# Three of four query and key chunks of the first block computed by seven half-size products each

## The chip, the core and the metric

The kernel runs on one core of one Trainium2 chip. Its engines are PE (TensorE, the matrix engine), DVE (VectorE), ACT (ScalarE), POOL (GpSimd) and SP (SyncE, which here only issues DMAs); each runs its own list of instructions in order, and semaphores tie them together. The metric is the device time of one launch in microseconds (us), the median of several runs.

## The reference, cut to what matters

The kernel computes two transformer blocks on 512 tokens of width 1024, in float32. The first is differential attention followed by a mixture of experts, the second a Fourier and neighbourhood-attention mixer. The change touches the first projection of the first block:

```
xn = x * rsqrt(mean(x*x, -1) + 1e-6) * gain          # [512, 1024]
q, k, v = split(xn @ w_in, [1024, 2048])             # w_in [1024, 3072]
q = rmsnorm per head of 64 (q, q_gain) * 64**-0.5    # 8 heads x 2 x 64
k = rmsnorm per head of 64 (k, k_gain)
...
# in the second block, the same kind of product for its own input
sh, sc, g = split(silu(c) @ w_ada + b_ada)           # modulation, also computed early here
q, k, v, f_in, f_gate, na_gate = split(xn2 @ w_in2)
```

A chunk is 512 columns of `w_in`: two chunks are q (q0, q1), two are k (k0, k1), two are v.

## The kernel before, in words

The order of each engine's work is written out by hand; nothing is scheduled by a planner. `x` comes in four tiles of 128 tokens. PE transposes a tile (`h_transposes`), DVE copies it out of PSUM times the gain into `hT` (`h_copies`), and DVE, ACT and POOL work out the row factor `rstd` from the sum of squares (`norm1`, `norm1_power`). `hT` itself stays without `rstd`, which is applied to every product later.

The projection is 24 units (`unit(i)`), a unit being one chunk times one token tile: 8 matmuls of 128x128 by 128x512 into one of two PSUM banks called "mm" (L824). Units 0 to 15 are q and k, units 16, 17 the first of v; the other six are fed in between the steps of the attention. Behind each q or k unit ACT squares it (L1345), DVE sums the squares by head (L1693) and adds the epsilon (L1698, L1702), POOL takes the power -1/2 (L2288), DVE scales into `pd` (L1709), and behind the next unit PE transposes `pd` (`qkT`, L795) into one of two PSUM banks called "tp"; ACT copies that into `qT` or `kT` (L1356). The scheme of the two banks: whoever wants to write the n-th tile of a kind calls `claim`, which waits until tile n-2 was drained; the bookkeeping is `turn` and `book`.

Between the units lie six steps of the modulation of the second block: `ada_rows` (8 matmuls on a `w_ada` chunk of 2 MB, L856), which ACT copies out (L1369), and `ada` (4 small matmuls, L842), which DVE drains in `ada_out` (L1679, L1682). They use the same two tp banks as the transposes, and their places are two lists, `ADA_ROWS_AFTER` and `ADA_AFTER`. SP loads the `w_ada` chunks into ring slots 0 and 1 as these come free (L654).

The ring has six slots of 2 MB in SBUF. The six chunks of `w_in` fill them at the start (L630, L622).

The second block has the scheme that the change brings to the first. For five of its chunks (`SEVEN`) a product of 512x1024 by 1024x512 is done as seven products of half size (256x512 by 512x256, 8 matmuls of 128x128 by 128x256, L1197). DVE makes four sums of the left operand once (`row_sum`, L2060), four of each weight chunk (`half_sum`, L2049) and seven sums of the products (`block_sum`, L2073); ACT copies the first product out (L1584).

Of the kernel before, what the change touches and what calls it, by code (L numbers as in the profile page):

```python
# [7 lines left out]
ALU = mybir.AluOpType  # L8
# [52 lines left out]
W_IN, W_OUT, W_MOE = 0, 8, 10  # L61
# [6 lines left out]
ADA_ROWS_AFTER = [6, 8, 9, 11, 12, 14]  # L68
ADA_AFTER = [7, 9, 10, 12, 13, 15]
# [106 lines left out]
SUMS_BEHIND = [None, 1, 4, 3, 5, 6, 7]  # L176
Q_BLOCKS = [(1, 1), (0, 0), (0, 1), (1, 0)]
HEADS_T_BEHIND = {("v", 2): 5, ("q", 6): 6, ("q", 7): 7, ("u", 1): 8, ("u", 2): 9}
# [44 lines left out]
def build(nc, ctx, A, out):  # L223
# [3 lines left out]
    def sem(name):  # L227
# [74 lines left out]
    ada_rows = s_buf[:, 0]  # L302
# [13 lines left out]
    lam_in = s_buf[:, 1, 0, 0:4 * DH].rearrange("p (n d) -> p n d", n=4)  # L316
    lam_pr = s_buf[:, 1, 1, 0:2 * DH].rearrange("p (n d) -> p n d", n=2)
# [31 lines left out]
              ("ng", buf_d[:, 2048:4096]), ("fg", ring[:, 3, 2048:4096]))}  # L349
# [44 lines left out]
    for i in range(UNITS_FIRST):  # L394
        book("mm", "proj", i)
    for i in range(UNITS_FIRST):
        if i < TT - 1:
            book("tp", "hT", 2 * i + 2)
            book("tp", "hT", 2 * i + 3)
        if 1 <= i <= QK_CHUNKS * TT:  # L400
            book("tp", "qkT", i - 1)
        if i in ADA_AFTER:
            book("tp", "ada", ADA_AFTER.index(i))
        if i in ADA_ROWS_AFTER:
            book("tp", "ada_rows", ADA_ROWS_AFTER.index(i))
# [56 lines left out]
    for what in SEVEN:  # L462
# [23 lines left out]
    slot_of, loads = {}, [9, 9, 10, 10, 9, 9]  # L486
# [12 lines left out]
    def w_half(what):  # L499

        w = ring[:, slot_of[source[what]][0], :].rearrange("p (k n) -> p k n", k=KD)
# [4 lines left out]
    def bank(j, step):  # L506

        n = 7 * j + step - 1
        b = sc_before % 2
# [91 lines left out]
    product_done = sem("product_done")  # L601
    s_ready, t_ready = sem("s_ready"), sem("t_ready")
    p1_copied = sem("p1_copied")
    sum_done = sem("sum_done")
# [14 lines left out]
    def _(sp):  # L619
# [29 lines left out]
        def load_ada(c):  # L649
            if c >= 2:  # L650
                filled(sp, "tp", turn["tp", "ada_rows", c - 2])
            else:
                filled(sp, "mm", turn["mm", "proj", (c + 1) * TT - 1])
            sp.dma_start(ring[:, c % 2, :].rearrange("p (k n) -> p k n", k=KD),  # L654
# [13 lines left out]
        for c in range(2, ADA_CHUNKS):  # L668
            load_ada(c)
# [1823 lines left out]
```

## Time and profile before

| | us |
|---|---|
| three timed runs | 955.51, 960.42, 960.25 |
| median | 960.25 |
| the profiled execution, its own time | 955.6 |
| its span in the trace | 953.5 |
| PE busy | 928.2 (97%) |
| DVE busy | 315.1 (33%) |
| ACT busy | 217.2 (23%) |
| POOL busy | 124.2 (13%) |

The profiled execution agrees with the fastest timed run; two of the three timed runs lie 4.7 to 4.9 us above it. Times inside the trace are us from the start of the span. In the trace one matmul of float32 is two records ("x16" are 8 matmuls), a matmul's record is longer than the distance to the next since they are pipelined, so what a group costs PE is read from one start to the next. In the chain of waits each piece is given with what it really adds. The units of q, k and the first of v run from 8.8 to 163.6 us, the attention follows, then the experts (358 to 629 us), then the second block, whose seven-product stage runs from 684.5 to 807.7 us.

### The profile page before, as it was taken

How to read it: one execution, taken by the hardware profiler on the slowest of the kernel's cores; microseconds unless marked ns; L12 is line 12 of the kernel's file. 1: busy time of each engine (PE TensorE's matmuls, PEld its weight loads, DVE VectorE, ACT ScalarE, POOL GpSimd, SP SyncE). 2: the span in 40 equal slices, each digit the busy share in tenths (PEclk: the TensorE clock that was granted, in tenths of full speed). 3: DMA queues.
4: the chain of work that ended last, by engine and by line, in shares of the span. 5: the costliest groups of instructions: out<-in, count | busy, mean ns of one | idle time of the engine just before them, and what ended most of it. 6: DMA issues, size and time to landing. Idle time of an engine off the chain costs nothing.

```text
span 953.5 us, 12683 instructions
## 1 busy us (share of the span) xinstructions
PE 928.2 (97%) x5258; PEld 476.1 (50%) x5258; DVE 315.1 (33%) x744; ACT 217.2 (23%) x471; POOL 124.2 (13%) x123
## 2 busy tenths in 40 slices
PE   7999999989999999999999999999999999999998
PEld 3544444444555453333333333335588888755543
DVE  2321121345774462100110110037735533344422
ACT  2121121334554310010010010114202011632310
POOL 3222121000001201000000000023202122530000
PEclk9999999999999999999999999999999999999999
DMA  9927527306001628999999999971283103500002
GB/s 329 290 96 229 204 107 276 142 1 259 6 1 45 226 89 315 376 395 409 419 413 428 422 412 415 380 262 45 92 164 107 57 23 90 198 1 1 1 12 78
DMA packets 54233, 186.32 MB, mean 195 GB/s; under 512 B 13968, under 2 KB 14624, under 8 KB 47904
## 3 DMA queue, kind: packets, MB, share of 16 engines
q1 hardware_dynamic: 45776, 160.31, 45.1%
q0 software_dynamic: 4912, 18.36, 5.2%
q10 hardware_dynamic: 3488, 6.82, 1.9%
q8 instruction: 43, 0.70, 0.3%
q14 instruction: 14, 0.11, 0.0%
HBM read 168.70 MB, written 16.79 MB: 195 GB/s over the span
## 4 chain that ended last, share of the span: by engine, by line
PE 87%; DVE 4%; DMA 3%; ACT 2%; issue 1%; SPq 1%; POOL 1%; ACTq 0%; DVEq 0%; POOLq 0%
PE psum L1022 17%; PE psum L1197 13%; PE psum L824 12%; PE psum L1045 8%; PE psum L795 6%; PE psum L1209 6%; PE psum L922 6%; PE psum L871 4%; PE psum L883 2%; PE psum L900 2%; PE psum L1266 1%; PE psum L949 1%; PE psum L1139 1%; PE psum L1296 1%; PE psum L856 1%
## 5 line engine op out<-in xcount | busy, mean ns | idle before, releaser
L1022 PE MATMUL psum<-ring,buf_a 128*32 128x512 f32 x1536 | 167.5, 593 | 1.1 <-DVE buf_a L1940 1.1
L824 PE MATMUL psum<-ring,buf_b 128*128 128x512 f32 x288 | 130.5, 606 | 2.0 <-DMA ring<-in_da_w_in 2.0
L1022 PEld LDWEIGHTS psum<-ring,buf_a 128*32 128x32 f32 x1536 | 48.9, 110 | 110.2 <-issue 110.2
L824 PEld LDWEIGHTS psum<-ring,buf_b 128*128 128x128 f32 x288 | 54.1, 193 | 68.4 <-issue 65.9
L1045 PE MATMUL psum<-ring,buf_c 128*32 128x512 f32 x768 | 84.7, 593 | 0.0
L2288 POOL TENSOR_TENSOR qk_st<-qk_st,half 128x8 f32<-128x8 f32 x26 | 43.6, 1677 | 165.8 <-DVE qk_st L2020 68.6
L922 PE MATMUL psum<-ring,buf_b 128*128 128x512 f32 x128 | 59.8, 594 | 0.0
L1209 PE MATMUL psum<-ring,buf_b 128*128 128x512 f32 x128 | 56.2, 595 | 1.7 <-DVE buf_b L2258 1.5
L1962 DVE TENSOR_TENSOR buf_c<-buf_c,psum 128x512 f32<-128x512 f32 x12 | 13.1, 1092 | 121.6 <-PE psum L1022 61.6
L1045 PEld LDWEIGHTS psum<-ring,buf_c 128*32 128x32 f32 x768 | 23.8, 110 | 52.7 <-issue 52.7
L1940 DVE TENSOR_TENSOR buf_a<-psum,gain 128x512 f32<-128x512 f32 x24 | 15.5, 687 | 101.3 <-PE psum L795 101.3
L1388 ACT ACTIVATE s_buf<-s_buf,nmx 128x128 f32<-128x128 f32 (+3 forms) x64 | 35.4, 554 | 58.9 <-DVE nmx L1756 58.9
L871 PE MATMUL psum<-ring,buf_b 128*128 128x512 f32 x96 | 44.7, 598 | 2.6 <-DVE o_sb L1776 1.8
L1756 DVE CUSTOM_DVE_ANT_0 s_buf<-psum,g_x 128x128 f32<-128x128 f32 (+3 forms) x64 | 28.9, 489 | 45.8 <-PE psum L883 45.7
L1209 PEld LDWEIGHTS psum<-ring,buf_b 128*128 128x128 f32 x128 | 23.9, 190 | 31.9 <-issue 28.9
L2354 POOL DMA_INDIRECT buf_b<-xn_d,idx x12 | 11.4, 948 | 212.9 <-PE psum L795 194.8
L2073 DVE TENSOR_TENSOR s_buf<-s_buf,psum 128x512 f32<-128x512 f32 x31 | 21.3, 687 | 47.0 <-PE psum L1197 45.3
L1197 PE MATMUL psum<-ring,buf_a 128*128 128x256 f32 x160 | 35.8, 379 | 0.0
L1693 DVE TENSOR_REDUCE qk_st<-pT 128x8 f32<-128x512 f32 x16 | 11.0, 686 | 73.0 <-ACT pT L1345 73.0
L795 PEld LDWEIGHTS psum<-ident,pd 128*128 128x128 f32 x184 | 21.6, 141 | 26.2 <-issue 23.4
L1345 ACT ACTIVATE pT<-psum,rstd 128x512 f32<-128x512 f32 x16 | 11.0, 687 | 99.0 <-PE psum L824 99.0
L1197 PE MATMUL psum<-ring,buf_b 128*128 128x256 f32 x144 | 32.4, 379 | 0.0
(294 smaller groups left out, 1186.4 us busy)
## 6 DMA issues: line engine op xcount, KB each, us to landing
ring<-in_moe_w_gate SPq DMA_DIRECT2D x16, 2048.0 KB, 12.9
ring<-in_moe_w_up SPq DMA_DIRECT2D x16, 2048.0 KB, 12.9
ring<-in_moe_w_down SPq DMA_DIRECT2D x16, 2048.0 KB, 12.6
ring<-in_w_in SPq DMA_DIRECT2D x7, 2048.0 KB, 9.5
ring<-in_w_ada SPq DMA_DIRECT2D x6, 2048.0 KB, 8.1
ring<-in_da_w_in SPq DMA_DIRECT2D x5, 2048.0 KB, 20.3
y_d<-ring POOLq DMA_DIRECT2D x1, 5632.0 KB, 22.9
y_d<-buf_b ACTq DMA_DIRECT2D x11, 512.0 KB, 11.3
```

Source lines behind the costliest of these rows:

```text
L795: last = transpose(buf("tp", n)[:, g * P:(g + 1) * P], block_in, ident[:])
L824: last = mm(buf("mm", n), hT[:, k, t * P:(t + 1) * P], slot(W_IN + c)[:, k, :], start=(k == 0), stop=(k == KD - 1))
L871: last = mm(buf("mm", n), hT[:, k, t * P:(t + 1) * P], slot(W_IN + c)[:, k, :], start=(k == 0), stop=(k == KD - 1))
L922: last = mm(buf("mm", n), oT[:, k, t * P:(t + 1) * P], slot(W_OUT + c)[:, k, :], start=(k == 0), stop=(k == KD - 1))
L1022: last = mm(buf("mm", n)[rows, :], xgT[:, s % 4, k, rows], slot(moe_load(q, m, r))[:, k, :], start=(k == 0), stop=(k == KD - 1))
L1045: last = mm(buf("sc", n)[rows, m, :], hidT[:, s % 3, f * P + SUB * j:f * P + SUB * (j + 1)], slot(moe_load(q, 2, r), FC)[:, f, m * CH:(m + ...
L1197: last = mm(out_bank[:, a * 256:(a + 1) * 256], still, moving, start=(k == 0), stop=(k == KD // 2 - 1))
L1209: last = mm(buf("sc", n)[:, a, :], mixT[:, k, t * P:(t + 1) * P], w[:, k, :], start=(k == first), stop=(k == first + 3))
L1388: last = S.activation(sc, sc, ACT.Exp, bias=nmx[:, m % 2, c:c + 1], scale=-1.0, accum_out=den[:, m % 2, c:c + 1])
L1756: last = V.tensor_tensor_reduce(out=s_buf[:, b, c, 0:w], in0=buf("sc", n)[:, c, 0:w], in1=dist[:, 512 - w:512], scale=-2.0 ** -(h + 1), sc ...
L2073: V.tensor_tensor(two(part[out]) if dst is None else dst, two(part[left]), two(bank(j, step)), ALU.add).then_inc(sum_done, 1)
L2288: G.tensor_tensor(dst, src, half[:, 0:width], ALU.pow).then_inc(signal, 1)
```

## The change

Of the four q and k chunks the first (units 0 to 3) stays as it was. The other twelve units (q1, k0, k1) are replaced by seven products each, 21 in all, with the function of the second block, now called `seven_products(f, j)` with f = 0 for the first block. What follows from it:

- The products need the operand with `rstd` in it. So each tile of `hT` is scaled in place (`scale_rows`) once the unit that reads it is done. The factor has to lie along the free axis for that: DVE builds `ident * rstd` for the four tiles, and PE multiplies it by a matrix of ones, one matmul, behind unit 1. v needs no scale any more.
- DVE makes the sums, and squares, means and scales come at the end of a chunk, from SBUF.
- The transposes and the `ada` steps move behind products, by three new tables. The `w_ada` chunks go to ring slots 1 and 2 and are loaded from the end of the first seven products on; `w_out` goes to slots 0 and 3.
- In the first block the sums of q1 lie in `buf_d`, those of k0 and k1 in ring slot 0.
- The order of the seven products is new in both blocks: the two that need no sums first. The waits of the second block move with it (among them that of the loads of `v_win`, from the fourth product of the last chunk to the fifth).
- Two loads of expert weights change places: that of up matrix 0 is issued early, that of gate matrix 2 in its place.

```diff
-ADA_ROWS_AFTER = [6, 8, 9, 11, 12, 14]
-ADA_AFTER = [7, 9, 10, 12, 13, 15]
+ADA_ROWS_BEHIND = {("k0", 4): 0, ("k0", 7): 1, ("k1", 2): 2, ("k1", 4): 3, ("k1", 6): 4, ("unit", 16): 5}
+ADA_BEHIND = {("k0", 6): 0, ("k1", 1): 1, ("k1", 3): 2, ("k1", 5): 3, ("k1", 7): 4, ("unit", 17): 5}
-SEVEN = ("v", "q", "u", "ng", "fg")
+SEVEN = ("q1", "k0", "k1"), ("v", "q", "u", "ng", "fg")
-PRODUCTS = [("A11", "B11"), ("S2", "T2"), ("S1", "T1"), ("S3", "T3"), ("A12", "B21"), ("S4", "B22"), ("A22", "T4")]
+PRODUCTS = [("A11", "B11"), ("A12", "B21"), ("S2", "T2"), ("S1", "T1"), ("S3", "T3"), ("S4", "B22"), ("A22", "T4")]
+QK_T_BEHIND = {("q1", 2): [3], ("q1", 7): [4], ("k0", 1): [5], ("k0", 2): [6], ("k0", 3): [7], ("k0", 7): [8],
+               ("k1", 1): [9], ("k1", 2): [10], ("k1", 3): [11], ("k1", 7): [12], ("unit", 16): [13, 14],
+               ("unit", 17): [15]}
...
@@ SP
+        for c in range(ADA_CHUNKS):
+            if c == 0:
+                sp.wait_ge(product_done[0], 7)
+            elif c == 3:
+                sp.wait_ge(product_done[0], 14)
+            else:
+                filled(sp, "tp", turn["tp", "ada_rows", {1: 0, 2: 1, 4: 2, 5: 3}[c]])
...
-            sp.wait_ge(product_done, 7 * 4 + (4 if c < TT - 1 else 6))
+            sp.wait_ge(product_done[1], 7 * 4 + (5 if c < TT - 1 else 6))
...
@@ PE
+        for i in (0, 1, 2, 3, 16, 17):
+            if i == 16:
+                for j in range(len(SEVEN[0])):
+                    landed(W_IN + 1 + j)
+                    seven_products(0, j)
+                pe.wait_ge(sum_done[0], 7 * 2 + 5)
...
+            if 1 <= i < TT:
+                qk_transposes(i - 1)
+            if i == 1:
+                pe.wait_ge(diag_ready, 1)
+                mm(bank(0, 0, 6), ones[:], part["c11"], start=True, stop=True).then_inc(rstd_row_ready, 1)
+            work_behind("unit", i)
...
@@ ACT, behind each chunk's products
+            act.wait_ge(sum_done[0], 7 * j + 6)
+            first_squares(4 * j + 6, part["c12"])
+            copies_behind(what, 7)
+            act.wait_ge(sum_done[0], 7 * j + 7)
+            first_squares(4 * j + 7, part["c21"])
...
@@ DVE
+        ada_in = {("k0", 7): 0, ("k1", 0): 1, ("k1", 2): 2, ("k1", 6): 3, ("k1", 7): 4}
...
+        for i in range(TT):
+            if i < TT - 1:
+                h_copies(i + 1)
+                if i < 2:
+                    norm1(i + 1)
+            if i == 1:
+                norm1(TT - 1)
+                for n in (1, 2, 3):
+                    half_sum(0, 0, n)
+            if i == 2:
+                scale_rows(0)
+            if i == TT - 1:
+                scale_rows(TT - 1)
+                row_sum(0, 1)
+                row_sum(0, 2)
+            first_mean(i)
+            if i == 1:
+                for t in range(TT):
+                    dve.wait_ge(rstd_ready, t + 1)
+                    last = V.tensor_scalar(part["c11"][:, t * P:(t + 1) * P], ident[:], rstd[:, t:t + 1], None, ALU.mult)
+                last.then_inc(diag_ready, 1)
+            if i == 2:
+                scale_rows(1)
+            first_scale(i, buf("mm", turn["mm", "proj", i]))
+            if i == 2:
+                scale_rows(2)
...
+        for j in range(3):
+            at = 4 * j + 4
+            half_sum(0, j, 4)
...
+            block_sum(0, j, 5)
+            first_mean(at)
+            block_sum(0, j, 6)
+            ada_sums(SEVEN[0][j], 6)
+            first_scale(at, part["c22"])
+            first_mean(at + 1)
...
+            first_scale(at + 1, part["c11"])
+            first_mean(at + 2)
+            block_sum(0, j, 7)
+            first_scale(at + 2, part["c12"])
+            ada_sums(SEVEN[0][j], 7)
+            first_mean(at + 3)
+            first_scale(at + 3, part["c21"])
```

Three places of the order, as it stands in the program. The first is DVE around unit 1, before. L1660 are the copies of tile 2 into `hT`, L1654 the mean for `rstd`, L1693 and L1698 the sum of the squares of unit 1, L1709 its scaling:

```order
L1660 TENSOR_TENSOR buf_b<-psum,gain 128x4x128 x2
L1654 TENSOR_SCALAR ms<-ssq 128x1
L1693 TENSOR_REDUCE qk_st<-pT 128x8
L1698 SCALAR_TENSOR_TENSOR qk_st<-qk_st,q_scale 128x8
L1709 SCALAR_TENSOR_TENSOR pd<-psum,rstd,qk_st 128x512
```

The same stretch of DVE after, where L1801 is `half_sum` and L1890 the diagonal:

```order
L1750 TENSOR_TENSOR buf_b<-psum,gain 128x4x128 x2
L1744 TENSOR_SCALAR ms<-ssq 128x1 x2
L1801 TENSOR_TENSOR buf_d<-ring 128x1024
L1801 TENSOR_TENSOR buf_d<-ring,buf_d 128x1024
L1801 TENSOR_TENSOR ring<-ring 128x4x256
L1832 TENSOR_REDUCE qk_st<-pT 128x8
L1843 SCALAR_TENSOR_TENSOR qk_st<-qk_st,q_scale 128x8
L1890 TENSOR_SCALAR s_buf<-ident,rstd 128x128 x4
L1858 SCALAR_TENSOR_TENSOR pd<-psum,rstd,qk_st 128x512
```

Three weight sums and the four pieces of the diagonal have come in ahead of the scaling. On PE, the rows between unit 1 and unit 2 after (before, L937 was not there), with what each waits for:

```order
L928 MATMUL psum<-ring,buf_b 128x512 x2
L813 MATMUL psum<-ident,pd 128x128 [waits tp_free0,mm_free0]
L813 MATMUL psum<-ident,pd 128x128 x3
L937 MATMUL psum<-s_buf,ones 128x512 [waits diag_ready]
L928 MATMUL psum<-ring,buf_b 128x512 [waits tp_free0,mm_free0]
```

The matmul of ones stands ahead of unit 2 and waits for the diagonal. The third place is PE where k0 ends and k1 begins, after: L902 are products, L813 the transposes of piece 8, L865 is `ada_rows` 1, L851 `ada` 0:

```order
L851 MATMUL psum<-o_sb,g_x 128x2 [waits fold_ready,tp_free1,tp_free0]
L851 MATMUL psum<-o_sb,g_x 128x2 x3
L902 MATMUL psum<-ring,buf_b 128x256 [waits t_ready0,p1_copied0]
L902 MATMUL psum<-ring,buf_b 128x256 x7
L813 MATMUL psum<-ident,pd 128x128 [waits tp_free0,qk_scaled]
L813 MATMUL psum<-ident,pd 128x128 x3
L865 MATMUL psum<-ring,o_sb 32x512 [waits ada_landed0,tp_free1]
```

and DVE in the same stretch, after. L1826 is `block_sum`, L1861 `first_scale`, L1832 with L1846 `first_mean`, L1769 `ada_out`:

```order
L1832 TENSOR_REDUCE qk_st<-pT 128x8 [waits sq_ready]
L1846 TENSOR_SCALAR qk_st<-qk_st 128x8 [waits dve_done]
L1826 TENSOR_TENSOR s_buf<-s_buf,psum 128x512 [waits product_done0]
L1861 TENSOR_TENSOR pd<-s_buf,qk_st 128x512 [waits tp_full0,qk_rstd_ready]
L1769 TENSOR_TENSOR mod_sh<-psum,b_ada 128x2x4 [waits tp_full1]
L1832 TENSOR_REDUCE qk_st<-pT 128x8 [waits sq_ready]
```

The drain of `ada` 0 (L1769), which frees the tp bank that `ada_rows` 1 claims, stands behind the scaling of the third piece of k0. Before, on PE, an `ada` and the next step in its bank had a whole unit of eight matmuls between them:

```order
L842 MATMUL psum<-o_sb,s_buf 128x2 [waits fold_ready,tp_free0]
L842 MATMUL psum<-o_sb,s_buf 128x2 x3
L824 MATMUL psum<-ring,buf_b 128x512 [waits mm_free0,w_landed2]
L824 MATMUL psum<-ring,buf_b 128x512 x7
L795 MATMUL psum<-ident,pd 128x128 [waits tp_free1,mm_free1]
L795 MATMUL psum<-ident,pd 128x128 x3
L856 MATMUL psum<-ring,o_sb 32x512 [waits ada_landed1,tp_free0]
```

There DVE drained `ada` 0 ahead of everything else of the next unit.

## Rows read from the trace of the kernel before

**Rows 1.** The page's first part: engine, busy us (share), instructions.

```profile
PE 928.2 (97%) x5258; PEld 476.1 (50%) x5258; DVE 315.1 (33%) x744; ACT 217.2 (23%) x471; POOL 124.2 (13%) x123
```

**Rows 2.** The chain of waits, first units: start us, us, what.

```profile
8.76 7.97 PE psum L824 x12
...
27.07 0.44 PE psum L795 x4
27.50 5.15 PE psum L824 x12
...
42.99 6.87 PE psum L824 x16
```

**Rows 3.** Windows: stretch, length, busy by engine, PEclk, DMA share, GB/s.

```profile
9.00:11.00 2.00, 2.00 (x3) 0.94 (x4) 0.15 (x1) 0.00 (x0) 1.78 (x10) 1.00 1.06 416
42.99:163.59 120.60, 119.42 (x421) 55.84 (x421) 22.24 (x51) 22.31 (x36) 23.29 (x15) 1.00 0.51 169
```

**Rows 4.** The chain of waits, seven-product stage.

```profile
742.11 65.61 PE psum L1197 x304
```

**Rows 5.** DVE in order of time, around unit 1: start us, us, line, operation.

```profile
24.95 1.29 DVE L1660 TENSOR_TENSOR buf_b<-psum,gain 128x512 f32<-128x512 f32 x2 [1.46 <-PE psum L795]
26.15 0.14 DVE L1654 TENSOR_SCALAR ms<-ssq 128x1 f32<-128x1 f32 x1
```

**Rows 6.** DVE in order of time, sums of the second block.

```profile
692.21 1.22 DVE L2049 TENSOR_TENSOR buf_d<-ring 128x1024 f32<-128x1024 f32 x1
693.46 1.23 DVE L2049 TENSOR_TENSOR buf_d<-ring,buf_d 128x1024 f32<-128x1024 f32 x1
694.61 1.22 DVE L2049 TENSOR_TENSOR ring<-ring 128x1024 f32<-128x1024 f32 x1
695.74 0.68 DVE L2073 TENSOR_TENSOR s_buf<-s_buf,psum 128x512 f32<-128x512 f32 x1
...
723.13 1.48 DVE L2073 TENSOR_TENSOR s_buf<-s_buf,psum 128x512 f32<-128x512 f32 x2 [1.63 <-PE psum L1197]
724.53 1.22 DVE L2049 TENSOR_TENSOR ring<-ring 128x1024 f32<-128x1024 f32 x1
725.66 0.68 DVE L2019 TENSOR_REDUCE qk_st<-pT 128x8 f32<-128x512 f32 x1
726.38 0.17 DVE L2020 TENSOR_SCALAR qk_st<-qk_st 128x8 f32<-128x8 f32 x1
...
728.30 0.69 DVE L2027 TENSOR_TENSOR pd<-s_buf,qk_st 128x512 f32<-128x512 f32 x1 [1.03 <-POOL qk_st L2288]
...
731.54 0.69 DVE L2027 TENSOR_TENSOR pd<-s_buf,qk_st 128x512 f32<-128x512 f32 x1 [0.82 <-POOL qk_st L2288]
```

**Rows 7.** DVE, a small operation: group by line, busy us, mean ns.

```profile
L2012 DVE TENSOR_SCALAR buf_b<-psum,mod_g,mod_sh 128x128 f32<-128x128 f32 x16 | 5.4, 404 | 0.0
```

**Rows 8.** The chain of waits, modulation steps among the units.

```profile
85.37 8.15 DMA ring<-in_w_ada
93.52 0.14 issue
...
103.08 0.79 PE psum L842 x8
```

**Rows 9.** PE in order of time, around the same steps.

```profile
91.65 0.95 PE L842 MATMUL psum<-o_sb,s_buf 128*128 128x2 f32 x8
93.65 1.92 PE L856 MATMUL psum<-ring,o_sb 128*32 128x512 f32 x16 [1.05 <-DMA ring<-in_w_ada]
```

**Rows 10.** ACT in order of time, behind unit 16.

```profile
156.33 0.69 ACT L1334 ACTIVATE buf_a<-psum,rstd 128x512 f32<-128x512 f32 x1 [6.93 <-PE psum L824]
156.91 0.68 ACT L1356 ACTIVATE buf_d<-psum,qk_gain 128x512 f32<-128x512 f32 x1
```

**Rows 11.** SP's DMA issues in order of time, the loads of `v_win`.

```profile
797.47 15.41 SPq L763 DMA_DIRECT2D buf_a<-v_d  x32
```

**Rows 12.** DMA issues, stretch 790 to 830 us: count, KB each, us to landing.

```profile
buf_a<-v_d SPq DMA_DIRECT2D x32, 64.0 KB, 1.9
```

**Rows 13.** The chain of waits, first product that reads `v_win`.

```profile
820.37 1.09 PE psum L1296 x16
```

More of the change, by code:

```diff
@@ L399, in build @@
             book("tp", "hT", 2 * i + 3)
-        if 1 <= i <= QK_CHUNKS * TT:
+        if i >= 1:
             book("tp", "qkT", i - 1)
[L402 to L405, printed above, removed]
+    for what in SEVEN[0]:
+        for step in range(1, 8):
+            book_behind(what, step)
+    for i in (16, 17):
+        book_behind("unit", i)
     for s in range(ATTENTION_STEPS):
@@ new lines, in ada_copy, with copies_behind, first_squares @@
+        def ada_copy(c):
+            n = turn["tp", "ada_rows", c]
+            filled(act, "tp", n)
+            if c >= 2:
+                filled(act, "tp", turn["tp", "ada", c - 2])
+            drain(S.copy(ada_rows[c % 2], buf("tp", n)), "tp", n)
+        def copies_behind(*place):
+            for j in QK_T_BEHIND.get(place, []):
+                qk_copy(j)
+            if place in ADA_ROWS_BEHIND:
+                ada_copy(ADA_ROWS_BEHIND[place])
+        def first_squares(j, src):
+            if j >= 2:
+                act.wait_ge(qk_ms_ready, j - 1)
+            if j < TT:
+                act.wait_ge(rstd_ready, j + 1)
+                ins = S.activation(pT[:, j % 2, :], src, ACT.Square, scale=rstd[:, j:j + 1])
+            else:
+                ins = S.activation(pT[:, j % 2, :], src, ACT.Square)
+            ins.then_inc(sq_ready, 1)
@@ new lines, in _ @@
+        for i in range(TT):
+            n = turn["mm", "proj", i]
+            filled(act, "mm", n)
+            first_squares(i, buf("mm", n))
+            if i >= 1:
+                qk_copy(i - 1)
+        act.wait_ge(second_loaded, 10 * 16)
+        act.wait_ge(pool_consts, 2)
+        S.activation(cond_pad[:, :, 0:2], cond[:], ACT.Silu).then_inc(cond_ready, 1)
+        for j, what in enumerate(SEVEN[0]):
+            act.wait_ge(product_done[0], 7 * j + 1)
+            if j == 0:
+                act.wait_ge(rstd_row_ready, 1)
+            else:
+                act.wait_ge(qk_scaled, 4 * (j - 1) + 2)
+            S.copy(part["c11"], bank(0, j, 1)).then_inc(p1_copied[0], 1)
+            for step in (1, 2, 3, 4):
+                copies_behind(what, step)
+            act.wait_ge(sum_done[0], 7 * j + 4)
+            first_squares(4 * j + 4, part["c22"])
+            copies_behind(what, 5)
+            act.wait_ge(sum_done[0], 7 * j + 5)
+            first_squares(4 * j + 5, part["c11"])
+            copies_behind(what, 6)
+            act.wait_ge(sum_done[0], 7 * j + 6)
[3 more added lines that the diff above has]
+            first_squares(4 * j + 7, part["c21"])
@@ L1371, in norm2_squares @@
+        for i in (16, 17):
+            v_copy(i)
+            copies_behind("unit", i)
         def norm2_squares(t):
@@ new lines, in row_sum @@
+        def row_sum(f, n):
+            left, right, op = {1: ("A21", "A22", ALU.add), 2: ("S1", "A11", ALU.subtract),
+                               3: ("A11", "A21", ALU.subtract), 4: ("A12", "S2", ALU.subtract)}[n]
+            if n == 1 and f == 0:
+                dve.wait_ge(h_scaled, TT)
+            elif n == 1:
+                drained(dve, "tp", turn["tp", "x3T", 2 * (TT - 1)])
+                drained(dve, "tp", turn["tp", "x3T", 2 * (TT - 1) + 1])
+            elif n in (2, 4):
+                dve.wait_ge(s_ready[f], 1 if n == 2 else 2)
+            V.tensor_tensor(x_half[f"S{n}"], x_half[left], x_half[right], op).then_inc(s_ready[f], 1)
@@ new lines, in _, with block_sum @@
+        two = lambda ap: ap.rearrange("p (t n) -> p t n", t=2)
+        def block_sum(f, j, n, dst=None):
+            left, step, out = SUM_OF[n]
+            dve.wait_ge(product_done[f], 7 * j + step)
+            if n == 1:
+                dve.wait_ge(p1_copied[f], j + 1)
+            elif n in (2, 4):
+                dve.wait_ge(sum_done[f], 7 * j + n - 1)
+            V.tensor_tensor(two(part[out]) if dst is None else dst, two(part[left]), two(bank(f, j, step)),
+                            ALU.add).then_inc(sum_done[f], 1)
```

545 lines of the change are left out of this document (283 added, 262 removed).

## The prediction

> **What bounds the kernel now.** First the page's busy times: PE is busy 928.2 us, 97% of the span, no other engine over a third [rows 1]. So a change pays what it takes off PE's list, less what PE then waits for. Second the chain of waits over the first 60 us: it is PE and nothing else, unit behind unit with four transposes of 0.44 us between them, and a unit of eight matmuls costs 6.87 us [rows 2]. Third the window over units 4 to 17: 120.60 us, PE busy in 119.42 of them, DVE in 22.2, ACT in 22.3, POOL in 23.3 [rows 3]. All helpers have room there, but their work on one unit is a chain (square, sum, power, scale), and the changed order makes PE wait for ends of such chains. So fourth I read DVE in order of time, once where unit 1 ends [rows 5], once in the second block, where the scheme already runs [rows 6]. The sum is made against the profiled execution, 955.6 us (span 953.5), 4.65 us under the median of the runs, 960.25. Two of three timed runs lie at the upper level, and nothing in one trace says which comes; I add the difference found in the trace to the median. About 0.5%, 4.8 us, is what can be told from no change, and it is also the distance of the two levels.
>
> **What PE is relieved of.** Twelve units at 6.87 are 82.4 us. In the second block 19 products run in one piece of 65.61 us, 3.453 each, with no wait [rows 4]; 21 of them are 72.5 us. Gain 9.9 us. The sixteen transposes, six `ada_rows` (1.92) and six `ada` (0.79) stay [rows 8, 9]. New is one matmul of ones, 128x512: a sixth of 5.15, 0.86 us [rows 2], 1.0 with the change of operands around it. The wait for the third `w_ada` chunk, 1.2 us from 92.45 (91.65 + 0.79) to 93.65 [rows 8, 9], goes: it came from a load of 8.15 us issued late behind small loads; in the new order the first load starts at the end of the seventh product of q1 and is used four products, three transposes, some 15 us later, and each later one has at least 8.7 us, against 8.15. What is late next there is DVE, below.
>
> **First wait: the diagonal behind unit 1.** PE ends unit 1 and its transposes at 27.07 + 0.44 = 27.50 [rows 2] and then, ahead of unit 2, waits for four diagonal pieces. DVE's list: copies of tile 2 from 24.95, the mean at 26.15, a second such mean, so free at 26.3 [rows 5]. Then three weight sums, which take 3.53 us from the first start to the next instruction in the second block (692.21 to 695.74) [rows 6]: 29.9. Their chunk must have landed; I take it as landed, since chunk 1 is behind only 4 MB in SP's queue, and if it is late the wait grows. Then the sum of unit 1's squares, 0.72 to the next instruction, and that one, 0.1: 30.7 [rows 6]. The diagonal's four operations of 128x128 are not in the trace; nearest are the 0.40 us of a TENSOR_SCALAR of the same shape out of PSUM [rows 7] and the 0.17 of one of 128x8 [rows 6]. Four give 0.7 to 1.6; I take 1.0, nearer the small one, since the input is in SBUF. PE goes on at 31.7: **4.2 us** idle (3.9 to 4.8). Queued behind the waiting matmul are unit 2 and all else on PE, so nothing covers it. The sums could have waited: their user is the third product, 20 us later.
>
> **Second wait: the tp bank between k0 and k1.** `ada_rows` 1 claims the bank of `ada` 0, which DVE drains behind the scaling of k0's third piece. Count from the end of k0's seventh product. The fifth ended 7.8 us earlier (two products and one `ada` with 0.9). DVE then does two block sums, 1.40, one weight sum, 1.13 (723.13 to 724.53 to 725.66), a block sum of 0.6, and starts the mean of the first piece at -4.6 [rows 6]. Mean to second instruction 0.72, from there to the scaling 1.92 (726.38 to 728.30), where POOL's power is waited for, and from scaling to scaling 3.24 (728.30 to 731.54) [rows 6]. So the pieces are scaled at -2.0, +1.2 and +4.5, the drain of `ada` 0 ends at +5.3. PE arrives at +0.5, behind the transposes of piece 8: **4.8 us** idle. Bounds: 3.8, if each piece goes 0.3 us quicker, to 6, if POOL or ACT are late once. ACT makes it no shorter: its copy of `ada_rows` 1 stands ahead of the last squares, which only delays piece 11, needed 15 us later.
>
> **Small ones.** Behind k1's second product `ada_rows` 2 claims the bank of `ada` 1, drained behind a weight sum that itself waits for that product: 1.2 + 0.15 against 0.44 of transposes, 0.9 us. Behind unit 16, `ada_rows` 5 needs the first of two transposes copied by ACT, which first copies v: 0.6 and 0.7 [rows 10] against 0.87 on PE, 0.4 us. The other places have cover. The transposes of q1's first piece come 0.3 us after its scaling by the same count; that is thin, and a slip there costs what it slips. `scale_rows` and `row_sum`, 1.2 us each, end at about 51.4, the third product starts at 55.5. DVE's whole load per chunk is about 16 us of 24.
>
> **The second block.** PE has no wait in the seven-product stage [rows 4], so putting the sum-free products first can gain nothing there. It moves the 32 `v_win` loads one product, 3.45 us, later: 797.47 + 3.45 + 15.41, and 1.9 to land, is 818.2 [rows 11, 12]; the product that reads them starts at 820.37 [rows 13]. 2.1 us are left, cost 0. The swap of two expert loads changes nothing: the last of the four gate matrices is issued where it was.
>
> **Sum.** -9.9 + 1.0 + 4.2 + 4.8 + 0.9 + 0.4 - 1.2 = +0.2 us. Everything behind follows PE and only shifts. On the profiled execution 955.8, on the median **960.4 us**. The change gives PE ten microseconds and takes them back in two waits.
>
> **Rivals.** (A) The sum holds. 50%, 960.4.
>
> (B) PE's clock falls in the new idle stretches. The granted clock is 1.00 of full in every row, the 2.4 GHz level [rows 3]. Yet at the start, after PE had stood for 2 us, twelve records took 7.97 us, and the same twelve at 27.50 took 5.15 [rows 2], and from 9 to 11 us only three were begun [rows 3]: PE ran at the pace of the 1.2 GHz level, whatever the column says. The price of one such stretch is 2.8 us. Here PE would stand for 4.2 and 4.8 us, longer than anywhere in this trace once it had begun. For: that start. Against: no row shows a fall after dense work, for want of such a gap. One fall gives 963.2, two 966.0; this is the side on which the kernel is slower, and it decides if the records behind the gaps are 0.86 us apart. 27% together, a third of it for two. The Trainium skill (TensorE: Matmul & The Clock Gate, HAM oscillation) says that a matmul kernel whose waits for data are long enough falls back to the half rate after each of them and pays the warm-up again; by that rule both gaps are candidates, and no run here shows it yet.
>
> (C) One of the two waits is not there, since ada 0 is drained earlier than I count or the weight sums run in DVE's gap ahead of unit 1's end. For: DVE is idle 1.5 us there [rows 5]. Against: the written order. One gone is 955.6 to 956.2, both gone 951.4. 15% together, 3% for both.
>
> (D) The products don't run back to back in the first block, or `v_win` comes late: the 0.3 and 2.1 us of room are used up. The change then doesn't do what it says at its place; up to 2 us, 961 to 962.5. 8%.
>
> **Range and chances.** From (C) with one wait gone and some more, to (B) with two falls: 952 to 966.5. Faster by over 0.5% needs under 955.4: most of (C) and a share of (A) if the runs fall at the lower level: 14%. Slower by over 0.5%, over 965.1: two falls, one fall with a late helper, or the level of the runs: 19%. The rest, 67%, can't be told from no change.
>
> **What would show it.** In the changed kernel PE should stand behind unit 1 from 27.5 to about 31.7, ended by DVE's TENSOR_SCALAR into `s_buf`; and about 4.8 us ahead of the second `ada_rows`, ended by DVE's small sum into `mod_sh`. 21 products should cost 3.45 us each, and the attention should start at about 163.8 where it did at 163.59. A first gap under 2 us, or none ahead of the second `ada_rows`, would make the forecast wrong to the fast side; a pace of 0.86 us a record behind a gap, or waits at `qk_scaled` behind most products, to the slow side.

## The result and the profile after

The changed kernel takes 961.3 us (median of 12 runs, 960.59 to 961.75). The kernel before, run beside it, takes 955.85 us (12 runs, 953.42 to 961.43). The ratio is 1.0049, interval 1.0031 to 1.0068: half a per cent slower, at the edge of what I called no change. The time forecast, 960.4, lies 0.9 us from the time measured, but the difference forecast, +0.2 us, does not: it is +5.5 us on the medians and +5.6 us between the profiled executions (961.18 against 955.6). The median of 960.25 that I added the difference to came from three runs, two of which lay at an upper level of the kernel before; with more runs that level proves to be the rarer one (17 of 91 runs of the kernel before beside the experiments, all at 960.4 us or more; the 24 runs of the changed kernel lie within 1.6 us of each other). Two single slow runs, 1382 us of the first experiment and 1959 us of the kernel before beside it, stand outside these counts and all ratios.

The page after, first part, and its line of granted clock over 40 slices of 24 us:

```profile
span 959.1 us, 13033 instructions
PE 925.4 (96%) x5404; PEld 505.0 (53%) x5404; DVE 349.2 (36%) x789; ACT 217.8 (23%) x474; POOL 124.9 (13%) x123
PEclk9999899999999999999999999999999999999999
```

PE's busy time fell by 2.8 us only [rows 1], where 9.9 less 1.0 were expected: part of what is busy there is busy at a slower clock. One digit of the clock line is an 8. Before, all were 9.

The chain of waits after, from the transposes in unit 1 on (start us, us, what; it answers to [rows 2]):

```profile
24.98 0.02 issue
25.00 1.29 DVE buf_b L1750 x2
...
29.94 0.61 DVE qk_st L1832
...
30.65 0.88 DVE s_buf L1890 x4
31.53 0.04 issue
31.57 2.08 PE psum L937 x2
33.65 5.75 PE psum L928 x12
...
49.73 6.91 PE psum L902 x32
```

DVE is now on the chain: the sums of weights, the squares' sum, the four diagonal pieces, and then the matmul of ones (L937) at 31.57, where I had counted 31.7. But L937 takes 2.08 us, not 1.0, and the twelve records behind it (L928, L824 before) take 5.75, not 5.15 [rows 2]. Products follow at 6.91 for two, 3.455 each, as forecast.

PE in order of time after, with the idle time before a piece and what ended it, at the four new waits and at one that was there before:

```profile
31.57 2.08 PE L937 MATMUL psum<-s_buf,ones 128*128 128x512 f32 x2 [4.02 <-DVE s_buf L1890]
33.44 5.96 PE L928 MATMUL psum<-ring,buf_b 128*128 128x512 f32 x12
39.23 1.04 PE L813 MATMUL psum<-ident,x 128*128 128x128 f32 x8
...
108.80 3.64 PE L865 MATMUL psum<-ring,o_sb 128*32 128x512 f32 x16 [4.87 <-DVE mod_sh L1769]
112.37 4.13 PE L902 MATMUL psum<-ring,buf_b 128*128 128x256 f32 x16
116.34 0.60 PE L813 MATMUL psum<-ident,pd 128*128 128x128 f32 x4
...
122.75 1.92 PE L865 MATMUL psum<-ring,o_sb 128*32 128x512 f32 x16 [1.03 <-DVE mod_sh L1769]
...
157.93 1.92 PE L865 MATMUL psum<-ring,o_sb 128*32 128x512 f32 x16 [0.39 <-ACT buf_d L1403]
...
208.41 3.43 PE L951 MATMUL psum<-ring,buf_b 128*128 128x512 f32 x4 [1.80 <-DVE o_sb L1994]
```

The four waits are where they were forecast and as long: 4.02 (4.2), 4.87 (4.8), 1.03 (0.9), 0.39 (0.4). What was not in the sum is beside three of the idle times: `ada_rows` (L865) takes 3.64 us behind the wait of 4.87 and 1.92 behind the two short ones, and in the attention four records of v's projection (L951) take 3.43 us, where the kernel before had the same wait of 1.80 us and then 1.98:

```profile
203.97 1.98 PE L871 MATMUL psum<-ring,buf_b 128*128 128x512 f32 x4 [1.80 <-DVE o_sb L1776]
```

Windows of the changed kernel (stretch, length, busy PE, PEld, DVE, ACT, POOL, then PEclk, DMA share, GB/s; they answer to [rows 3], where PEclk is 1.00):

```profile
20.00:27.00 7.00, 7.00 (x24) 3.48 (x23) 3.60 (x8) 0.10 (x1) 2.22 (x2) 1.00 1.05 388
27.00:32.00 5.00, 0.98 (x6) 0.74 (x5) 4.45 (x9) 1.26 (x2) 3.40 (x3) 0.93 1.05 387
31.00:32.00 1.00, 0.43 (x1) 0.43 (x2) 0.52 (x3) 0.00 (x0) 1.00 (x1) 0.66 1.06 391
32.00:34.00 2.00, 2.00 (x3) 0.75 (x3) 0.75 (x1) 0.00 (x0) 0.46 (x1) 0.50 1.05 385
34.00:36.00 2.00, 2.00 (x5) 0.91 (x4) 0.00 (x0) 0.00 (x0) 0.00 (x0) 0.82 1.05 386
36.00:100.00 64.00, 63.95 (x297) 49.39 (x296) 37.54 (x51) 12.79 (x20) 10.00 (x7) 1.00 0.38 106
100.00:112.00 12.00, 7.13 (x36) 3.83 (x35) 5.09 (x12) 1.32 (x2) 4.73 (x3) 0.77 0.00 0
112.00:114.00 2.00, 2.00 (x10) 1.44 (x7) 0.34 (x1) 1.11 (x2) 0.00 (x0) 0.69 0.27 29
114.00:200.00 86.00, 83.91 (x382) 49.34 (x381) 25.08 (x103) 22.44 (x63) 10.25 (x7) 1.00 0.65 238
200.00:210.00 10.00, 8.20 (x28) 3.51 (x28) 4.07 (x18) 4.97 (x17) 0.00 (x0) 0.94 0.01 2
210.00:215.00 5.00, 5.00 (x17) 2.26 (x16) 2.20 (x9) 1.35 (x5) 0.00 (x0) 0.78 0.00 0
```

The granted clock falls to 0.50, the 1.2 GHz level, at the first wait. It fell before the matmul of ones began: the mean from 31 to 32 us is 0.66, which takes 0.68 us at 0.50, and L937 is there only from 31.57 on. The clock is also below 1.00 at the second wait and behind the one that ends at 208.41. By 36, 114 and 215 us it is back.

From these rows the difference of the two profiled executions comes out term by term. Waits 4.02 + 4.87 + 1.03 + 0.39 = 10.3; one of 0.2 at 74.4 us; the matmul of ones at full clock 0.9; the fall at the first wait 1.65 (from the wait's end to the next transposes 39.23 - 31.57 = 7.66, where runs without a fall, below, have 6.0 to 6.1); at the second 2.1 (116.34 - 108.80 = 7.54 against 5.42); in the attention 1.65 (from the end of this wait to the end of the next one 227.87 - 208.41 = 19.46 against 221.78 - 203.97 = 17.81; the pieces behind the four records are slow too); less 9.9 for the products, 1.05 for the DMA wait at 93.65 that is gone [rows 9], and 0.55 in the mixer, where PE's wait for a piece of DVE was 1.1 and not 1.67. The sum is +5.3, measured +5.6.

The second block's products, from the chain after (they answer to [rows 4]): they start 6.15 us later than before and what follows them, too, starts 6.15 later, so nothing was won or lost there.

```profile
690.82 6.91 PE psum L902 x32
...
698.16 41.44 PE psum L902 x192
...
826.53 1.09 PE psum L1345 x16
```

### The profile page after: what moved, and what is told of

It is laid out like the page before. It is cut to its first block, busy times and chain, and to the rows that moved or that the text cites. A ratio compares the mean times of both kernels' runs of the same rounds, so it can differ in the third digit from the quotient of the medians.

```text
span 959.1 us, 13033 instructions
## 1 busy us (share of the span) xinstructions
PE 925.4 (96%) x5404; PEld 505.0 (53%) x5404; DVE 349.2 (36%) x789; ACT 217.8 (23%) x474; POOL 124.9 (13%) x123
## 4 chain that ended last, share of the span: by engine, by line
PE 87%; DVE 6%; DMA 2%; ACT 2%; POOL 2%; issue 1%; ACTq 0%; DVEq 0%; SPq 0%; POOLq 0%
PE psum L902 19%; PE psum L1104 17%; PE psum L1127 8%; PE psum L813 6%; PE psum L1259 6%; PE psum L1004 6%; PE psum L951 5%; PE psum L928 5%; PE psum L965 2%; PE psum L982 2%; PE psum L1315 1%; PE psum L1031 1%; PE psum L1221 1%; PE psum L865 1%; POOL qk_st L2466 1%
## 5 line engine op out<-in xcount | busy, mean ns | idle before, releaser
L902 PE MATMUL psum<-ring,buf_a 128*128 128x256 f32 x320 | 71.5, 381 | 0.0
L902 PEld LDWEIGHTS psum<-ring,buf_a 128*128 128x128 f32 x320 | 60.0, 190 | 10.3 <-issue 2.5
L902 PE MATMUL psum<-ring,buf_b 128*128 128x256 f32 x288 | 65.2, 382 | 0.0
L1004 PE MATMUL psum<-ring,buf_b 128*128 128x512 f32 x128 | 59.8, 594 | 0.0
L902 PEld LDWEIGHTS psum<-ring,buf_b 128*128 128x128 f32 x288 | 54.3, 191 | 9.5 <-issue 2.5
L1826 DVE TENSOR_TENSOR s_buf<-s_buf,psum 128x512 f32<-128x512 f32 x52 | 35.3, 685 | 65.4 <-PE psum L902 60.3
L1259 PE MATMUL psum<-ring,buf_b 128*128 128x512 f32 x128 | 56.2, 595 | 1.7 <-DVE buf_b L2436 1.5
L951 PE MATMUL psum<-ring,buf_b 128*128 128x512 f32 x96 | 46.2, 615 | 2.5 <-DVE o_sb L1994 1.8
L928 PE MATMUL psum<-ring,buf_b 128*128 128x512 f32 x96 | 46.3, 635 | 2.1 <-DMA ring<-in_da_w_in 2.1
L1259 PEld LDWEIGHTS psum<-ring,buf_b 128*128 128x128 f32 x128 | 23.9, 190 | 31.9 <-issue 28.9
L813 PEld LDWEIGHTS psum<-ident,pd 128*128 128x128 f32 x184 | 21.3, 141 | 21.8 <-issue 17.5
L928 PEld LDWEIGHTS psum<-ring,buf_b 128*128 128x128 f32 x96 | 19.2, 206 | 25.6 <-issue 23.1
```

Source lines behind the costliest of these rows:

```text
L813: last = transpose(buf("tp", n)[:, g * P:(g + 1) * P], block_in, ident[:])
L902: last = mm(out_bank[:, a * 256:(a + 1) * 256], still, moving, start=(k == 0), stop=(k == KD // 2 - 1))
L928: last = mm(buf("mm", n), hT[:, k, t * P:(t + 1) * P], slot(W_IN + c)[:, k, :], start=(k == 0), stop=(k == KD - 1))
L951: last = mm(buf("mm", n), hT[:, k, t * P:(t + 1) * P], slot(W_IN + c)[:, k, :], start=(k == 0), stop=(k == KD - 1))
L1004: last = mm(buf("mm", n), oT[:, k, t * P:(t + 1) * P], slot(W_OUT[c])[:, k, :], start=(k == 0), stop=(k == KD - 1))
L1259: last = mm(buf("sc", n)[:, a, :], mixT[:, k, t * P:(t + 1) * P], w[:, k, :], start=(k == first), stop=(k == first + 3))
```

## The experiments

My theory after the result: each of the two long waits costs its length and then a fall of TensorE's granted clock, because TensorE stands. The rivals: the slow records belong to the new instructions (the matmul of ones, with its operands) and not to standing; or a wait that is taken away comes back elsewhere.

**The second wait alone.** VectorE's drain of `ada` 0 one place earlier:

```diff
-        ada_in = {("k0", 7): 0, ("k1", 0): 1, ...
+        ada_in = {("k0", 6): 0, ("k1", 0): 1, ...
```

> The changed kernel with one entry of VectorE's table of ada's drains moved: the drain of ada's column 0 stands behind block sum 6 of k0, ahead of the scaling of k0's third piece, and no longer behind block sum 7. Theory A (a wait costs its length and then a fall of TensorE's granted clock): the idle stretch of 4.87 us at 108.80 goes, and with it the slow stretch behind it (3.64 us for ada's four matmuls and 4.06 for sixteen matmuls of a product, together 2.2 more than at the full clock), so 7 us less than the changed kernel: about 954.3. Rival B (the wait costs its length alone): 4.9 less, about 956.4. Rival C (the same wait comes back at the next claim of the small bank, or DVE is late elsewhere): 0 to 2 less, 959 to 961.

Measured: 953.66 us (12 runs), ratio to before 0.9967 (0.9939 to 0.9995). That is 0.95 below the 954.61 of before beside it, where the changed kernel was 5.45 above its own: 6.4 us won (theory A 7, rival B 4.9). The wait of 4.87 is gone from the trace, those of 1.03 and 0.39 stand, and between 100 and 114 us the clock is 1.00. The first wait is as it was:

```profile
31.87 2.08 PE L937 MATMUL psum<-s_buf,ones 128*128 128x512 f32 x2 [4.02 <-DVE s_buf L1890]
33.74 6.00 PE L928 MATMUL psum<-ring,buf_b 128*128 128x512 f32 x12
```

**The first wait alone.** The matmul of ones one unit later:

```diff
-            if i == 1:
+            if i == 2:
                 pe.wait_ge(diag_ready, 1)
```

> The changed kernel with the matmul by ones, which waits for VectorE's diagonal, one unit later on TensorE (behind unit 2 and not behind unit 1). Theory A (wait and clock): the idle stretch of 4.02 us at 31.57 goes and the 1.75 us that the twelve matmuls behind it took longer, so 5.8 less than the changed kernel: about 955.5. Rival B (length alone): 4.0 less, about 957.3. Rival C (TensorE idles elsewhere, since what hangs on the mean, the first products among it, comes a unit later): 961 or more, with a new wait ahead of the first product.

Measured: 953.02 us (12 runs), 0.9969 (0.9946 to 0.9993), 1.6 below before: 7.0 us won, where theory A said 5.8 and rival B 4.0. The rest may be the third fall: in this profiled execution the records behind the wait of 1.80 us in the attention take 1.98 us, not 3.43, and its mean clock, 0.998, is that of nine of the twelve runs. Rival C is out: the first product does not wait.

**Both.** The two edits together.

> Both edits: the drain of ada's column 0 behind block sum 6, and the matmul by ones behind unit 2. Theory A: the two savings add, 7.0 + 5.8 = 12.8 less than the changed kernel, about 948.5, below the kernel before by some 7. Rival B (idle lengths alone): 8.9 less, about 952.4. Rival C (the time so gained is given back where a later stage waits for weights or for v): no more than the 6 by which the changed kernel is behind, 955 or above.

Measured: 945.96 us (6 runs), 0.9887 (0.9847 to 0.9928); on another chip 946.54 (6 runs), 0.9894 (0.9859 to 0.9929):

> The run with both waits removed, once more on another chip for a narrower interval: 946, or 0.989 of the kernel before. Below the run with short filler by the lengths of the two waits, 8.9, and 0 to 1.5 more where one of the two had a fall in the attention.

This beats both kernels, the one before by 1.1% by the ratio and by 8.6 us by both pairs of medians (954.61 and 955.17 beside them). Between executions with a mean clock of 1.00 only, without any fall on either side, the difference is 7.7 to 7.8 us (953.75 and 954.21 for the kernel before): the rest of the 8.6 is that some runs of the kernel before have falls and these have none. It is lower than the 948.5 expected; the granted clock of all twelve runs is 1.00 on average, so the fall in the attention, 1.65 us, was absent too. Windows of the run with both edits, to be laid beside those of the changed kernel:

```profile
27.00:32.00 5.00, 5.00 (x19) 2.68 (x18) 3.99 (x10) 0.00 (x0) 2.29 (x2) 1.00 1.05 387
32.00:34.00 2.00, 2.00 (x9) 0.99 (x8) 0.91 (x2) 0.23 (x1) 0.00 (x0) 1.00 1.06 391
...
100.00:112.00 12.00, 10.97 (x67) 8.35 (x66) 3.45 (x6) 2.54 (x5) 2.19 (x2) 1.00 0.99 351
```

PE is busy in all 5.00 us from 27 to 32 (0.98 in the changed kernel). The 1.03 us missing from 100 to 112 are the third wait, which ends at 108.30 here.

**And the third wait.** The drain of the next `ada` ahead of the half sum:

```diff
+            ada_sums(SEVEN[0][j], 0)
             half_sum(0, j, 4)
-            ada_sums(SEVEN[0][j], 0)
```

> As the run with both edits, and VectorE's drain of the next ada column stands ahead of the half sum of the next chunk's sums, which takes the wait of 1.03 us at 122.75 away. Theory A: 1.0 less than the run with both edits, about 947.5, without a clock fall there (the granted clock was full behind that wait). Rival B: no difference, since the half sum is then late for its product and TensorE waits there for as long: 948.5. This is the version that should beat both kernels, by about 8 us the kernel before.

Measured: 946.96 us (6 runs), 0.9891 (0.9849 to 0.9932), not below the run before it. The wait of 1.03 is gone, and the attention's wait starts 1.0 us earlier once the start of the kernel is subtracted (the first twelve records took 8.05 us here and 6.85 there); but five of six runs have a mean clock of 0.998, and the profiled one shows the fall behind the wait of 1.80 us (3.27 us for the four records). So the 1 us is won where it was expected and given back at another place, which is in some executions so and in others not. My "947.5, beats both by about 8" is right in size, the reason for preferring it to the version with two edits is not borne out.

**Standing alone, nothing else changed.** The kernel before, with TensorE held behind unit 1 by additions on VectorE that nothing uses; three or five of them:

```diff
+            if i == 1:
+                pe.wait_ge(gap_over, 1)
...
+                for n in range(3):   # or 5
+                    last = V.tensor_tensor(buf_d[:, 816 * n:816 * n + 816], x[:, 0, 0:816], x[:, 0, 0:816], ALU.add)
+                last.then_inc(gap_over, 1)
```

> The kernel before with a wait put in: TensorE, behind unit 1 of the q and k chunks (27.3 us), waits for three additions of 128x816 on VectorE that nothing uses (about 1 us each by the 686 ns of a 128x512 row), an idle stretch of about 2.1 us; no other work is added to TensorE. Theory A (idle costs its length and then a clock fall): 2.1 us and up to 1.8 us more, 3 to 4 us above the kernel before, with a granted clock under 1.00 just behind the stretch; a shorter stretch may stay without a fall. Rival B (length alone): 2.1 above.

> The same with five additions: an idle stretch of about 3.9 us at 27.3, as long as the first one of the changed kernel (4.02). Theory A: 3.9 + 1.8 = 5.7 us above the kernel before, with the granted clock near 0.5 for two microseconds behind the stretch. Rival B (length alone; what was slow in the changed kernel came of its new instructions and not of the idleness): 3.9 above, and the twelve matmuls behind the stretch at their 5.15 to 5.3 us.

Measured: 956.97 us with three (12 runs; before beside it 954.8), 1.0022 (0.9999 to 1.0045); 962.15 with five (6 runs), 1.0067 (1.0043 to 1.009). PE in order of time, three additions first, then five:

```profile
28.65 5.42 PE L825 MATMUL psum<-ring,buf_b 128*128 128x512 f32 x12 [1.60 <-DVE buf_d L1696]
33.91 1.04 PE L796 MATMUL psum<-ident,x 128*128 128x128 f32 x8
```

```profile
30.34 6.94 PE L825 MATMUL psum<-ring,buf_b 128*128 128x512 f32 x12 [3.44 <-DVE buf_d L1696]
37.12 1.04 PE L796 MATMUL psum<-ident,x 128*128 128x128 f32 x8
```

And a window of the run with five, just behind the stretch of 3.44 us:

```profile
32.00:34.00 2.00, 2.00 (x4) 0.86 (x3) 0.75 (x1) 0.00 (x0) 0.81 (x1) 0.64 1.05 386
```

The stretches came out shorter than I had written, 1.60 and 3.44 us. Behind 1.60 us the clock stays at 1.00 and the twelve records take their usual time; the median is 2.2 above before. Behind 3.44 us the window from 32 to 34 us has a granted clock of 0.64 and the same twelve records take 1.5 us longer (37.12 - 30.34 = 6.78 against 33.91 - 28.65 = 5.26). No new instruction stands there, so the rival that blamed the matmul of ones is out. The medians leave something open. With three additions 2.2 above before stand against 1.60 of standing, less 1.05 for the DMA wait at 93.65 [rows 9], which is absent here; with five, 7.35 against 3.44 + 1.5 - 1.05 = 3.9. In the traces the attention's wait of 1.80 us ends later by 0.5 and 3.8 us, as those sums say. For five additions a fall in the attention may be in the medians: the other five runs have a mean clock of 0.996, which the first experiment's profiled execution has with two falls. That would be 1.65 us. For three it can't be: the runs with a mean clock of 1.00 (eight of them, ten of the kernel before) differ by 2.7 us too. So about 2 us are unexplained in both; the profiled execution with five (965.48) does not help, since it has a disturbance of its own, which the last section tells of. The 1.5 us of the fall are read from the trace and do not hang on this.

**The order of the products alone.** The kernel before with the sum-free products first in the second block, and the waits that go with it:

```diff
-PRODUCTS = [("A11", "B11"), ("S2", "T2"), ("S1", "T1"), ("S3", "T3"), ("A12", "B21"), ...
+PRODUCTS = [("A11", "B11"), ("A12", "B21"), ("S2", "T2"), ("S1", "T1"), ("S3", "T3"), ...
```

> The kernel before with the new order of the seven products alone (sum-free ones first, and the waits, transposes and accumulations that go with it); the first block's q and k stay with eight-step units. Theory A: TensorE waits nowhere in the second block's products in either order, so nothing changes: within 0.5 us of the kernel before. Rival B: the new order hides a cost of its own (or gives a gain) of 1 to 2 us that the changed kernel's other terms covered.

Measured: 954.42 us (12 runs), 0.9993 (0.9979 to 1.0007). Nothing, as theory A said.

**Both waits kept, TensorE not standing.** Matmuls whose result nobody reads, put in front of each wait of the changed kernel. First eight in front of the first wait, and ten in front of the second; the changed kernel again beside them.

```diff
             if i == 1:
+                for _ in range(8):
+                    mm(bank(0, 0, 6), hT[:, 0, 0:P], slot(W_IN)[:, 0, :], start=True, stop=True)
                 pe.wait_ge(diag_ready, 1)
...
+                if c == 1:
+                    pe.wait_ge(sum_done[0], 7 + SUMS_BEHIND[1])
+                    for _ in range(10):
+                        mm(bank(0, 2, 1), hT[:, 0, 0:P], hT[:, 0, :], start=True, stop=True)
                 claim(pe, "tp", n)
```

> The changed kernel with eight matmuls of 128x512 whose result nobody reads put in front of TensorE's wait for VectorE's diagonal (behind unit 1). TensorE is still held until 31.6 us, but works for 3.4 of the 4.0 us instead of standing. Theory A (it is the standing that makes the granted clock fall): the clock stays at 1.00 behind the wait, the twelve matmuls of unit 2 take 5.2 and not 5.75 us, the ones matmul 0.9 and not 2.08: 1.6 to 1.75 less than the changed kernel, about 959.6, though work was added. Rival B (what is slow behind the wait comes of the new matmul by ones and its operands): no gain, 961.3. Rival C (the filler's end comes later than VectorE's diagonal, or its eight matmuls take more than the wait covers): slower than the changed kernel.

> The same, and ten such matmuls (4.3 us) in front of the second wait (4.87 us, for the bank that VectorE drains after k0), written to the bank of the next product. Theory A: both falls go, 1.7 + 2.2 = 3.9 less than the changed kernel, about 957.4, with both waits still there; the granted clock is 1.00 from 20 to 120 us. Rival B: 961.3. Against the run with both waits removed this leaves what the waits cost by their length, 8.9 us.

> The changed kernel itself once more, beside the two runs with filler on the same chip, so that a difference of 1.7 us can be told: 961.3 by its first runs, with three to four falls of the clock (mean clock 0.993 or 0.991).

Measured: 960.43 us with the first filler, 963.01 with both, 961.41 without (12 runs each). I had the filler's size wrong: a matmul of this size is two records of 0.43 us, and I had counted one. The filler was longer than the waits, 6.87 us against 4.02 and 8.68 against 4.87. From the transposes ahead of it to the instruction that had waited it is 7.31 us and not 4.61, and 9.11 and not 5.47, so 2.7 and 3.6 us more are on the path. That is rival C, and it happened. Still the first of the two is 1.0 us faster than the changed kernel with 2.7 us more on its path. So, once more, with four and five:

> Filler that fits into the waits: in the runs before, each filler matmul took 0.86 us (two records of 0.43), so eight lasted 6.87 us and ten 8.75, longer than the waits of 4.02 and 4.87. Now four (3.4 us) stand in front of the first wait and five (4.3 us) in front of the second. Both waits keep their ends. Theory A (standing makes the clock fall): the stretch from the end of the first wait to the end of unit 2's twelve matmuls takes 6.0 us and not 7.8 to 8.9, ada's four matmuls behind the second wait 1.9 and not 3.6, and the kernel is 3.5 to 5 below the changed kernel's 961.4: 956.4 to 957.9. Rival B (no part of it is the clock's): 961.4.

Measured: 957.06 us (12 runs), 1.0006 (0.9983 to 1.003), 1.89 above before beside it, where the changed kernel was 5.84 above its own: 3.95 us won, though nothing was saved and nine useless matmuls were added. PE in order of time, and its windows:

```profile
25.75 3.60 PE L941 MATMUL psum<-ring,buf_b 128*128 128x512 f32 x8
29.94 1.12 PE L943 MATMUL psum<-s_buf,ones 128*128 128x512 f32 x2 [0.58 <-DVE s_buf L1896]
30.90 5.31 PE L932 MATMUL psum<-ring,buf_b 128*128 128x512 f32 x12
36.05 1.04 PE L813 MATMUL psum<-ident,x 128*128 128x128 f32 x8
...
105.61 1.92 PE L869 MATMUL psum<-ring,o_sb 128*32 128x512 f32 x16 [0.58 <-DVE mod_sh L1775]
107.47 3.72 PE L906 MATMUL psum<-ring,buf_b 128*128 128x256 f32 x16
111.03 0.60 PE L813 MATMUL psum<-ident,pd 128*128 128x128 f32 x4
```

```profile
27.00:32.00 5.00, 4.42 (x11) 1.82 (x10) 3.60 (x9) 0.00 (x0) 2.22 (x2) 1.00 1.05 387
...
100.00:112.00 12.00, 11.42 (x58) 6.70 (x56) 4.23 (x10) 2.58 (x5) 4.79 (x3) 1.00 0.25 84
```

The same instructions behind the same waits: 36.05 - 29.94 = 6.1 us here, 7.66 in the changed kernel; 111.03 - 105.61 = 5.42 here, 7.54 there. The waits end as late as there, 4.62 us behind the start of the transposes ahead of the first (4.61 there). The clock is 1.00. Nothing but the standing was taken away. This settles it for these two waits: the falls come of TensorE's standing, and they cost the changed kernel about 4 us of its 5.5 (1.65 + 2.1 by the traces). No filler was tried at the attention's wait.

## Why the time was right and the reasoning was not

**The products and what they relieve** held: 3.455 us each against 3.453, no wait between them, the DMA wait gone. The second block's new order is worth nothing that the traces show: what stands ahead of it and behind it is later by the same 6.15 us. The four waits held to within 0.2 us each. Counting DVE's list item by item from rows of another stage [rows 5, 6] was good enough to place a wait of 4.9 us at the end of a long chain: k0's first three pieces were to be scaled at -2.0, +1.2 and +4.5 us from the end of the seventh product (103.33) and were at 101.50, 104.74 and 107.98.

**The step that failed is the choice between rivals A and B.** I gave the sum of lengths 50% and a fall of the clock 27%. Both long waits had their fall. For B I had a row (twelve records at the half pace after TensorE had stood for 2 us at the kernel's start [rows 2, 3]), and I set against it only that no gap in dense work was to be seen. That absence was no evidence, since the change was about to make two gaps longer than any in the trace. The Trainium skill (TensorE: Matmul & The Clock Gate, HAM oscillation) says of a matmul kernel that waits for loads that each wait, if long enough, is followed by a cold start; the traces agree, here for waits for VectorE, in each of the profiled executions that has one of the two waits. The price was 2.8 us a fall, from the start of the kernel, where the wait stands in this line of the trace before:

```profile
8.76 7.97 PE L824 MATMUL psum<-ring,buf_b 128*128 128x512 f32 x12 [2.00 <-DMA ring<-in_da_w_in]
```

That row is not quite a fall: TensorE had begun only at 4.82 us, and the clock column reads 1.00 there, while it reads 0.50 at the waits. Measured: at the first wait 1.65 us in the profiled changed kernel, 1.7 with the second wait alone removed and 2.9 in the repeat of the changed kernel (39.38 - 30.51 = 8.87 against 6.0); at the second 2.1, in the repeat 2.7, with the first removed 1.6 and with the first filled 1.3; 1.5 behind the 3.44 us of the held kernel. So the same wait does not cost the same each time.

**A third fall was foreseen by no rival.** Behind the attention's wait of 1.80 us, which both kernels have, the clock fell in 7 of the 14 profiled executions and not in the others (of before itself no, of before with the new order yes: 3.68 us for the four records). It costs 1.6 to 1.7 us each time, counted to the end of the next wait of TensorE; what decides for it was not found. This is a part of a kernel's spread: runs of the kernel before with a mean clock of 0.998 have a median of 955.97 (24 runs), those at 0.999 or 1.000 have 954.1 (50 runs).

**And the base was wrong.** With two falls rival B gives 955.6 + 0.2 + 5.6 = 961.4 on the profiled execution, which was measured at 961.18. I had added 4.65 us to bring it to the median of three runs. That put A at 960.4, near the truth for no good reason, and B at 966.0, where nothing was. A wrong base of +4.4 and a missing clock cost of -5.4 cancelled. That B comes so near on the right base is luck in its turn: its 5.6 us for two falls were 3.75 for these two and 1.65 for the third, which it did not know. The chances for slower and same were shifted by the same error: on a base of 955.6, A would have been "no change" and B "slower by 0.6%".

**What the change could have been** is seen with both waits removed by moving one matmul and one small drain: 8.6 us less than before by the medians, 7.7 to 7.8 between executions without falls. The other terms leave -9.9 + 0.9 + 1.03 + 0.39 - 1.05 = -8.6. That the medians give the same is in part chance, since without falls 0.8 to 0.9 of it is missing; where, was not found.

## What to carry to other kernels

Work taken off the bounding engine is worth what it says only if the engine does not stand instead. Price a new wait of TensorE at its length and a fall of its clock (here 1.3 to 2.9 us for waits of 3.4 us and more), even if the trace before shows a full clock everywhere. Look at where the waiting instruction stands in its program order before giving up on a change: here a matmul one unit later and a drain one place earlier, with no work saved, turned +5.5 us into -8.6. And when the terms are read from one profiled execution, take its own time as the base (955.6 here, against a median of 955.85 over twelve runs); a median of three runs of a kernel with two levels (960.25) is no base.

## What the runs showed of the hardware

**Filler made the kernel faster.** Nine useless matmuls gave 4 us, as shown above; filler that outlasts its wait takes that back (963.01).

**Standing of 1.0 to 1.67 us was followed by no fall, of 1.80 us in 7 of 14 profiled executions, of 3.44 us and more in all.** These are the stretches that occur here (3.44, 4.02, 4.87 and 6.31 above), nothing more. The one of 1.80 us is a single place in the program.

**VectorE can be held up for microseconds by GpSimd.** This is the disturbance in the profiled execution with five additions, in the mixer's stage, far from the edit. VectorE there, then GpSimd:

```profile
838.77 7.01 DVE L2253 TENSOR_TENSOR o_sb<-ident,rden 128x1024 f32<-128x1024 f32 x1
```

```profile
829.90 14.80 POOL L2450 TENSOR_TENSOR ring<-ring,g_x 128x512 f32<-128x512 f32 x12
```

The multiplication of 128x1024 takes 1.23 us later in the same trace, where GpSimd is idle, and 7.01 here, where it ends 1.1 us after the last of GpSimd's multiplications (844.70). The same GpSimd multiplications run beside it in all 14 profiled executions; in the other thirteen it takes 1.23 to 2.38 us (2.38 in the kernel before). Which of the two waits differs. With five additions the eight GpSimd multiplications from 834.8 us on took 1.27 to 1.29 us each. In the kernel before with the new order VectorE took 1.24 us and one of GpSimd's 2.27. TensorE stood 6.31 us for the long one and its clock fell again (0.60 from 846 to 850 us). The Trainium skill (SBUF — State Buffer, Who interferes with whom) says that a VectorE instruction with two inputs in SBUF contends with a GpSimd instruction that reads SBUF, since its second input comes through the read interface they share. The rows agree in that one of the two is held up, and add that it can be VectorE several times in a row; no run took GpSimd's work away, so the cause is argued from these times. The 17 runs of the kernel before at 960.4 us and more have a mean clock of 0.993 to 0.996 and would fit this, 4.6 us of blocking and a fall; none of them was profiled, so that is a guess that fits and not shown.
